# A two-layer hybrid network in one kernel: S5 output matrices made later, first loads reordered, small S5 products split, shared expert by halves

## What is computed

```python
h = layer_norm(ALPHA * h + mixed @ w_out[layer], ln1_w[layer], ln1_b[layer])
ffn = moe(h, router_w[layer], ...)          # 64 experts, 8 per token, one shared expert
h = layer_norm(ALPHA * h + ffn, ln2_w[layer], ln2_b[layer])
```

```python
shared = (jax.nn.silu(xt @ sw_gate) * (xt @ sw_up)) @ sw_down
```

## Time and profile before

| | |
|---|---|
| median of 3 executions | 1323.59 us (1323.25 to 1326.84) |
| the profiled execution | 1326.38 us |
| its span, first to last instruction | 1324.7 us |
| TensorE busy | 1287.8 us, 97% |
| TensorE weight loads | 699.5 us, 53% |
| VectorE, ScalarE, GpSimd busy | 527.7, 187.4, 46.7 us |
| mean granted TensorE clock | 0.985 of full speed |
| moved by the transfers | 462.33 MB, mean 349 GB/s |

### The profile page before, as it was taken

One profiled execution on the slowest core, in us unless ns is written; L12 is line 12 of the kernel. 1 busy time (PEld: TensorE's weight loads), 2 busy tenths in 40 slices (PEclk: granted clock), 3 DMA queues, 4 the chain that ended last, 5 costly groups with the idle time before them and its releaser, 6 DMA issues.

```text
span 1324.7 us, 16993 instructions
## 1 busy us (share of the span) xinstructions
PE 1287.8 (97%) x6753; PEld 699.5 (53%) x6753; DVE 527.7 (40%) x1071; ACT 187.4 (14%) x314; POOL 46.7 (4%) x76
## 2 busy tenths in 40 slices
PE   8979999999999999999999999999999999999996
PEld 6845564445544454445476656454445544454443
DVE  6777543333333333333336136233333333333324
ACT  3122201111111111111031212011111111111111
POOL 6200100000000000000010001000000000000000
PEclk9989999999999999999998998999999999999999
DMA  7853849999999999999952169499999999999992
GB/s 236 245 229 145 350 200 408 421 422 422 422 422 421 423 422 422 422 422 421 376 184 83 33 252 421 166 402 420 421 422 423 422 422 422 422 423 422 421 421 113
DMA packets 77625, 462.33 MB, mean 349 GB/s; under 512 B 9680, under 2 KB 10896, under 8 KB 27152
## 3 DMA queue, kind: packets, MB, share of 16 engines
q1 hardware_dynamic: 77584, 461.74, 86.0%
HBM read 455.36 MB, written 6.36 MB: 349 GB/s over the span
## 4 chain that ended last, share of the span: by engine, by line
PE 92%; DVE 4%; DMA 3%; issue 1%; ACT 1%; SPq 0%; DVEq 0%; ACTq 0%
PE bank L1040 33%; PE bank L1070 17%; PE bank L971 10%; PE bank L992 9%; PE bank L615 4%; PE bank L625 4%; PE bank L945 2%; PE bank L673 2%; PE bank L687 2%; PE bank L1051 1%; DMA expert_weights<-s_rows 1%; PE bank L1004 1%; DVE expert_weights L1531 1%; PE bank L980 1%; DMA weight_ring<-in_w_in_even 1%; PE bank L795 1%
## 5 line engine op out<-in xcount | busy, mean ns | idle before, releaser
L1070 PE MATMUL bank<-expert_weights,hiddenT 128*64 128x512 f32 x1024 | 233.8, 598 | 2.0 <-DVE hiddenT L1807 2.0
L1040 PE MATMUL bank<-expert_weights,hT 128*64 128x512 f32 x1024 | 225.3, 592 | 0.0
L1040 PE MATMUL bank<-expert_weights,weight_ring 128*64 128x512 f32 x1024 | 225.2, 592 | 0.0
L1804 DVE TENSOR_TENSOR hidden<-silu_gate,bank 128x256 f32<-128x256 f32 x64 | 26.9, 421 | 330.0 <-ACT silu_gate L1262 330.0
L1040 PEld LDWEIGHTS bank<-expert_weights,weight_ring 128*64 128x64 f32 x1024 | 74.5, 137 | 145.2 <-issue 145.2
L1040 PEld LDWEIGHTS bank<-expert_weights,hT 128*64 128x64 f32 x1024 | 73.4, 137 | 145.3 <-issue 145.0
L1070 PEld LDWEIGHTS bank<-expert_weights,hiddenT 128*64 128x64 f32 x1024 | 68.2, 136 | 119.7 <-issue 110.7
L992 PE MATMUL bank<-onehot_r,h_top 128*128 128x256 f32 x512 | 125.5, 288 | 0.0
L992 PE MATMUL bank<-onehot_r,h_low 128*128 128x256 f32 x512 | 119.7, 277 | 0.0
L971 PE MATMUL bank<-y_top,onehotT_r 128*128 128x512 f32 x264 | 111.8, 423 | 0.0
L971 PE MATMUL bank<-y_low,onehotT_r 128*128 128x512 f32 x264 | 104.5, 396 | 0.0
(11 more groups left out here) (359 smaller groups left out, 1073.6 us busy)
## 6 DMA issues: line engine op xcount, KB each, us to landing
expert_weights<-in_exp_w_gate SPq DMA_DIRECT2D x128, 1024.0 KB, 11.1
expert_weights<-in_exp_w_up SPq DMA_DIRECT2D x128, 1024.0 KB, 13.9
expert_weights<-in_exp_w_down SPq DMA_DIRECT2D x128, 1024.0 KB, 13.2
weight_ring<-in_w_in_even SPq DMA_DIRECT2D x6, 2048.0 KB, 10.3
weight_ring<-in_w_out SPq DMA_DIRECT2D x4, 2048.0 KB, 7.4
weight_ring<-in_w_in_odd SPq DMA_DIRECT2D x4, 2048.0 KB, 10.1
s_c<-expert_weights SPq DMA_DIRECT2D x1, 3072.0 KB, 8.7
expert_weights<-s_c SPq DMA_DIRECT2D x1, 3072.0 KB, 10.9
```

Of the source, the lines that this page charges most:

```text
L1040: last_mm = nc.tensor.matmul(bank[6][a * CAP:(a + 1) * CAP, :].rearrange("p (w f) -> p w f", w=2), xq[:, c, s0:s0 + CAP], ew_gu(2 * u + a, c),
L1070: last_mm = nc.tensor.matmul(bank[b][a * CAP:(a + 1) * CAP, :], hm[:, j, a * CAP:(a + 1) * CAP], ew_d(2 * u + a)[:, j, half * 512:(half + ...
L1804: nc.vector.tensor_tensor(hslot[:, :], sg[:, :], bank[6][:, DE:2 * DE], ALU.mult)\
```

## The change

- In mix0 the first loads are x tile 0, wgate, cols0, x tile 1 (the last three on the semaphore of x tile 1, waited for at 48), then xb0 and k0, and only then the other three small loads, waited for at 48 where they are read. Four warm-up products stand behind the transposes.
- `dve_s5_matrices` is split: inputs stay, `dve_s5_outputs` stands behind log_a.
- In mix1 the banks are written out by hand. K leaves the list and has the semaphore `direct`.
- The `bu` products come in two halves, the first between the halves of u's second job, the second behind `ga`. In y, r0 stands between q = 1 and q = 2 of the part from the states, instead of behind keT; ScalarE's silu of r0 moves ahead of the gelu.
- Up's second half goes to bank 2, and the shared product is made in two halves, the first behind the combine weights and ahead of the ranks' evaluation; `shared_down` has j as outer loop.
- In the ending pairs the scatter of tile 1 stands behind the transposes of the hidden part.

```diff
-                eng.wait_ge(S["x_loaded1" if t else "x_loaded"], 16)
+                eng.wait_ge(*((S["x_loaded1"], 48) if t else (S["x_loaded"], 16)))
...
 def sp_mix0(sp):
-            for dst, src in ((wgate[:, :, 0:8], ...), (cols0[:, :], A["cols_even"]), (gated..., A["lru_wa"]...),
+            for name in ("xb0", "k0"):
+                ring_load(sp, ring_no[name])
+            for dst, src in ((gated..., A["lru_wa"]...),
                              (onehotT_f..., A["lru_wx"]...), (onehot_f[:, :], A["mlstm_norm_w"]...)):
                 sp.dma_start(dst, src).then_inc(M0["params"], 16)
-            for name in ("xb0", "k0"):
-                ring_load(sp, ring_no[name])
...
-            for t, name in enumerate(("x_loaded", "x_loaded1")):
-                sp.dma_start(h[:, t, :], A["x"][0, t * P:(t + 1) * P, :]).then_inc(S[name], 16)
+            sp.dma_start(h[:, 0, :], A["x"][0, 0:P, :]).then_inc(S["x_loaded"], 16)
+            for dst, src in ((wgate[:, :, 0:8], ...), (cols0[:, :], A["cols_even"]), (h[:, 1, :], A["x"][0, P:2 * P, :])):
+                sp.dma_start(dst, src).then_inc(S["x_loaded1"], 16)
...
 def dve_mix0(dve, chain):
             last.then_inc(M0["xc"], 1)
-            dve_s5_matrices(dve, chain)
+            dve_s5_inputs(dve, chain)
             dve.wait_ge(*B.full("cols"))
...
             nc.vector.tensor_tensor(V["rg"], V["rg"], L[:, 4, :]..., ALU.mult).then_inc(M0["log_a"], 1)
+            dve_s5_outputs(dve, chain)
...
 def pe_mix1(pe):
             ring_arrived(pe, "u1")
-            for i in range(2):
-                channel_major(pe, B, ring_view("u1"), "u", i)
+            channel_major(pe, B, ring_view("u1"), "u", 0)
+            channel_half(pe, B, ring_view("u1"), "u", 1, 0)
+            pe.wait_ge(M1["b_in"], 16)
+            pe.wait_ge(*B.read("u0"))
+            for j in range(4):
+                B.wait_free(pe, f"bu{j}")
+            state_inputs((0, 1))
+            channel_half(pe, B, ring_view("u1"), "u", 1, 1).then_inc(B.full_sem, 1)
             (the gate products ga)
+            pe.wait_ge(*B.read("u1"))
+            state_inputs((2, 3))
...
             pe.wait_ge(M1["states"], 1)
             for q in range(4):
+                if q == 2:
+                    ring_arrived(pe, "r1")
+                    token_major(pe, B, ring_view("r1"), "r", 0)
...
-            ring_arrived(pe, "r1")
-            token_major(pe, B, ring_view("r1"), "r", 0)
             pe.wait_ge(*B.read("keT"))
...
 def pe_moe(pe, l):
-                        last = nc.tensor.matmul(bank[w][:, j * SEQ:(j + 1) * SEQ], wv[:, c, j, :], hT[:, c, :],
+                        dst = bank[1 + j][:, 0:SEQ] if w else bank[0][:, j * SEQ:(j + 1) * SEQ]
+                        last = nc.tensor.matmul(dst, wv[:, c, j, :], hT[:, c, :],
...
-                        scatter(1 - u, False)
+                        scatter(1 - u, False, (0,) if ending else (0, 1))
                         (transposes of hidden)
+                        if ending:
+                            scatter(1 - u, False, (1,))
...
+        def shared_hidden(dve, l, j):
+            m = MO[l]
+            dve.wait_ge(m["sh_silu"], 1)
+            dve.wait_ge(m["sh_gu"], j + 2)
+            nc.vector.tensor_tensor(shid[l][:, j, :], sh_silu[l][:, j, :], bank[1 + j][:, 0:SEQ], ALU.mult)\
+              .then_inc(m["sh_hidden"], 1)
```

More of the change, by code:

```diff
@@ L603, in _, with warm_up @@
                     pool_moe(pool, int(st[-1]))
+        def warm_up(pe, count):
+            for _ in range(count):
+                nc.tensor.matmul(bank[7][:, 0:P], ident[:, :], ident[:, :], start=True, stop=True)
         def keep_clock(pe, b, count):
@@ L608, in keep_clock, with channel_half @@
                 nc.tensor.matmul(bank[b][:, 0:SEQ], ident[:, :], hT[:, 0, :], start=True, stop=True)
-        def channel_major(pe, B, w, name, i):
[L612 to L619, removed]
+        def channel_half(pe, B, w, name, i, a):
+            if a == 0:
+                B.wait_free(pe, f"{name}{i}")
+            for c in range(KC):
+                last = nc.tensor.matmul(B.tile(f"{name}{i}")[:, a * SEQ:(a + 1) * SEQ],
+                                        w[:, c, (2 * i + a) * P:(2 * i + a + 1) * P], hT[:, c, :],
+                                        start=(c == 0), stop=(c == KC - 1))
+            return last
+        def channel_major(pe, B, w, name, i):
+            channel_half(pe, B, w, name, i, 0)
+            channel_half(pe, B, w, name, i, 1).then_inc(B.full_sem, 1)
         def token_major(pe, B, w, name, t):
@@ L657, in pe_transposes @@
                         last.then_inc(B.full_sem, 1)
+            if not stage_no[st]:
+                warm_up(pe, 4)
             for b in range(4):
@@ L783, in pe_mix1 @@
             last.then_inc(B.full_sem, 1)
-            pe.wait_ge(M1["b_in"], 16)
             pe.wait_ge(*B.read("u1"))
[L787 to L799, removed]
+            state_inputs((2, 3))
             ring_arrived(pe, "qk1")
@@ L948, in pe_moe @@
                         continue
+                    last.then_inc(m["sh_gu"], 1)
                     pe.wait_ge(m["chosen"], 1)
@@ L957, in pe_moe, with scatter @@
                 last.then_inc(m["sh_gu"], 1)
-            def scatter(par, done):
-                for t in range(TT):
+            def scatter(par, done, tiles=range(TT)):
+                for t in tiles:
                     if done:
@@ L1000, in shared_down @@
             def shared_down(t):
-                for n in range(2):
-                    for j in range(JE):
+                for j in range(JE):
+                    if t == 0:
+                        pe.wait_ge(m["sh_hidden"], j + 1)
+                    for n in range(2):
                         last = nc.tensor.matmul(bank[2 * t + n][:, :], shid[l][:, j, t * P:(t + 1) * P],
@@ L1094, in _ @@
             pe.wait_ge(S["consts"], 1)
-            for _ in range(WARM):
-                nc.tensor.matmul(bank[7][:, 0:P], ident[:, :], ident[:, :], start=True, stop=True)
+            warm_up(pe, 10)
             pe.wait_ge(S["consts"], N_CONSTS)
@@ L1182, in act_mix1 @@
                 last = nc.scalar.copy(W["direct"][rows, :, :, 32 * j:32 * j + 32],
-                                      B.tile("K")[rows, 0:384].rearrange("p (q k c) -> p q k c", q=4, k=3))
-            last.then_inc(B.done["a"], 1)
+                                      bank[1][rows, 0:384].rearrange("p (q k c) -> p q k c", q=4, k=3))
             act.wait_ge(*B.full("low"))
@@ L1200, in act_mix1 @@
                 nc.scalar.copy(W["v"][:, t, :], B.tile(f"v{t}")[:, :]).then_inc(B.done["a"], 1)
+            act.wait_ge(*B.full("r0"))
+            nc.scalar.activation(W["og"][:, 0, :], B.tile("r0")[:, :], ACT.Silu).then_inc(B.done["a"], 1)
             act.wait_ge(*B.read("y1"))
@@ L1214, in act_mix1 @@
             act_copies(act, B, "keT", W["ke_tok"])
-            for t in range(TT):
-                act.wait_ge(*B.full(f"r{t}"))
-                nc.scalar.activation(W["og"][:, t, :], B.tile(f"r{t}")[:, :], ACT.Silu).then_inc(B.done["a"], 1)
+            act.wait_ge(*B.full("r1"))
+            nc.scalar.activation(W["og"][:, 1, :], B.tile("r1")[:, :], ACT.Silu).then_inc(B.done["a"], 1)
             for i in range(2):
@@ L1527, in dve_s5_powers, with dve_s5_inputs @@
               .then_inc(M1["powers"], 1)
-        def dve_s5_matrices(dve, chain):
+        def dve_s5_inputs(dve, chain):
             mul = lambda out, x, y: nc.vector.tensor_tensor(out, x, y, ALU.mult)
@@ L1545, in dve_s5_matrices, with dve_s5_outputs @@
                 dve.wait_ge(M1["bt"], half + 1)
+        def dve_s5_outputs(dve, chain):
+            mul = lambda out, x, y: nc.vector.tensor_tensor(out, x, y, ALU.mult)
             powers = pow5[:, 0:6, :].rearrange("p (k w) n -> p k w n", w=2)
```

51 lines of the change are left out of this document (28 added, 23 removed), and 8 rows, old and new, of tables (B1, odd_jobs).

## The result

The changed kernel takes 1309.74 us (median of 4 runs, 1308.31 to 1310.14) against 1323.42 for the kernel before, run beside it: ratio 0.9884, 95% interval 0.9870 to 0.9898. It is faster by 13.7 us by the medians; the forecast was 20.4 us and 1303.2, the range 1297 to 1311. The likeliest case (1299.5 to 1307.5) did not come; what came is the rival "o0 late" (1309). The profiled execution took 1309.92 us and spans 1308.2, 16.5 less than before.

What follows compares the result with a forecast made beforehand. The prediction took TensorE, busy 97% of the span, as the bound, with gains only outside the expert loop. Its terms, 3.0 + 10.9 - 0.8 + 1.9 + 1.6 + 1.4 + 3.1 + 4.6 - 3.0 - 2.3 = 20.4 us, gave 1303.2, range 1297 to 1311.

Steps and rivals of the forecast that it cites:

- likeliest case: Whole kernel: all terms come as summed, 1303.2 us, own range 1299.5 to 1307.5; chance 0.52.
- o0 late: Rival, first mixer: store and o0's load run end to end, wait 5 to 6 us plus clock fall, 1309; chance 0.14.
- The wait for o0: First mixer: o0's load behind the output matrices' store makes TensorE wait 0.8 us, bounds 0 and 6.
- Outputs behind the decay terms: First mixer: v1's 8.63 us wait for the gate columns' copy and 2.3 of half clock go; gain 10.9 us.
- First loads: Kernel start: reordered loads let xb0's products start at 13.8 instead of 16.88; gain 3.0 us, bounds 2.0 and 3.2.
- Shared halves: Shared expert in each expert layer: making its product by halves removes shared_down's 0.94 us wait; gain 1.9 us.
- scatter: Ends of expert layers: splitting the scatter covers four 0.5 us waits for hiddenT; gain 1.6 us.
- K: L772: taking K off the bank list shortens the 2.4 us wait for its copies; gain 1.4 us.
- Small products split: Second mixer: cutting both runs of 256 removes two stops, 3.1 us, and the half clock that follows, 4.6 us.
- Slower: Rival, expert loops: the stop enters every pass, 2.2 us each, 26 us in all, 1329; chance 0.02.
- r0 ahead: Second mixer: moving r0 earlier uncovers ScalarE's work before U; loss of 3.0 us idle and 2.3 of clock.
- kinder clock: Rival: no clock fall in front of U, and one untouched fall (2.9 us) stays away, 1298; chance 0.16.

Runs made afterwards that it cites:

- o0_first: Changed kernel with the load of o0 issued ahead of the wait for the output matrices and of their store; 1304.31 us, ratio 0.9845.
- outputs_alone: Kernel before with only the S5 output matrices moved behind the decay terms; 1317.99 us, ratio 0.9948.
- before_again: Kernel before, unchanged, profiled a second time; profiled at 1323.34 us, span 1321.6.
- bu_together: Version `both` with the 256 small S5 input products in one run again, behind ga; 1303.75 us, ratio 0.9858.
- r0_back: o0_first with r0 behind the keT transposes again, so y's 256 small products are one run; 1296.69 us, ratio 0.9800.
- bu_64_192: Version `both` with the 256 small input products cut 64 and 192 instead of 128 and 128; 1297.13 us, ratio 0.9806.
- shifted_192: bu_64_192 with 36 small identity products (72 passes and their loads) added at the head of the second mixer; 1310.04 us, ratio 0.9892.
- r1_split: Changed kernel with the first four chunks of product r1 placed ahead of U, the other four behind it; 1302.25 us, ratio 0.9833.
- both: Changed kernel with the edits of o0_first and r1_split together; 1297.94 us, ratio 0.9797.
- after_again: Changed kernel, unchanged, run and profiled a second time; 1309.39 us, ratio 0.9882, span 1306.6.
- loads_alone: Kernel before with only the new order of first loads, without the warm-up products; 1321.41 us, ratio 0.9985.

## Why the prediction was right and wrong, by its steps

The time lies inside the range, but not for the reason that the sum gave: the sum missed by 6.7 us (20.4 against 13.7), and what held was that most of the rival "o0 late" had been put into the range. With the sizes measured below (first loads, outputs, o0 as in the first profile, shared halves and scatter together, K, small products, r0) the forecast's sum is 3.0 + 11.05 - 7.5 + 4.0 + 1.24 + 7.5 - 6.0 = 13.3 us, near the 13.7 measured.

**The wait for o0: the term that failed.** The step said: "I take a wait of 0.8 us, bounds 0 and 6". It was 4.98 us and 2.5 of clock in the first profile, 2.10 and 0.1 in the second. Three things went into the miss. The load took 16.2 us from issue, where I had it land 13 to 14 us after: store and load together moved 5 MB, and that is halfway between my "run together" and my "laid end to end" (19 us from the load's issue). The rival's reason, end to end, is thus only half of it, though its price came true. DVE's outputs ended at 82.6, where the step had them (85.5 less the opening's 3.0), but TensorE had come 4.7 us nearer by v0, not 3.0, as the half clock at 63 us, which the step left in, wasn't there. That makes 2.2 to 3.2 us and 1.5 us. And I put no clock fall behind the wait, though a rival had it. That it was the load's place is shown by o0_first, that it comes with this edit alone by outputs_alone.

**Outputs behind the decay terms, 10.9 us.** Right in size: from v0's start to the S products the time fell by 11.05 us (24.78 to 13.73), and the copy of the gate columns was in time.

**First loads, 3.0.** The first xb0 product came 2.98 us earlier; alone, 2.0 us by the time of the whole kernel, with 3.0 inside its interval. The step counted on the gates at full clock. That alone gives nothing: in before_again and outputs_alone they had it, and xb0 was awaited 2.05 and 2.27 us and started at 16.49 and 16.43. It's the earlier issue of xb0's load that moved the start.

**Shared halves 1.9 and scatter 1.6.** Undone together they cost 4.0 us, against 3.5 taken.

**K, 1.4.** 1.24 us: the wait is 1.21 and was 2.45.

**Small products split, 3.1 and 4.6.** Right in size, 6.5 us for bu_together and 1.0 for y's stop in r0_back, wrong in reason. I wrote that "each run is shorter than what went through before a stop". bu_64_192 let a longer one through, and shifted_192 brought the stop back at a place worked out beforehand. The stops stand at borders in the instruction stream, 256 instructions apart, with 128 small products and their loads between two borders.

The traces show what TensorE waits for there, though the profile says only "issue". Transfers of instructions go over a queue of their own, 30 of 16 KB in each profile; those of the kernel before that start in 695 to 697 us (packets, MB, share of 16 engines):

```profile
q8 instruction: 1, 0.02, 2.8%
```

It runs from 695.36 to 696.26; TensorE stops at 695.64 and goes on at 697.80. All eleven stops in these profiles, six among the input products and five among y's, are like that: an instruction transfer starts 0.3 to 1.5 us before the stop, and TensorE goes on 1.3 to 1.6 us after it has landed. In bu_64_192 none starts during the run of 192. And none starts between 291 and 605 us of the kernel before, in the hardware loop of the first expert layer, so the rival "Slower", a stop in every pass, had nothing to wait for.

A rule that I had cited beside the sum says so: the Trainium skill, page Runtime: NRT & Kernel Launch, section Instruction fetch mechanics, has the sequencer fetch blocks of 256 while it runs the present one; the runs here agree on 256. The same section calls the cost of a border mostly hidden; here it is 0.9 to 2.2 us where the block is that short. A run of 128 can't hold a whole block but by chance, so the split avoids the stop by this too. That large products in a block prevent it rests on one case, bu_64_192. What decides when a transfer starts stays open: the block of 128 input products takes 3.9 us and had stops of 1.5 to 2.2, that of y's takes 1.95 and had 0.9 to 1.5.

**r0 ahead, -3.0 and -2.3.** The wait was 2.88 us in all three profiles with that order; the half clock 3.1 to 3.3, not 2.3. This part of the edit buys 1.0 us (y's stop) and costs 6.1; r0_back shows the balance, 5.2 us. With half of r1 in the gap (r1_split) both are had.

**The clock elsewhere.** The rival "kinder clock" had an untouched fall stay away at 2.9 us: before_again shows just that, in the kernel before. That fits the first profile's place, 3.0 us above the median (1326.38 against 1323.42), and so the difference between 16.5 us by the spans and 13.7 by the medians; which falls the other executions had, no trace shows.

The best here are `both`, bu_64_192 and r0_back, 1296.7 to 1297.9, ratios 0.9797 to 0.9806, which these runs can't tell apart: 2.0% faster than before, 0.8 points more than the change.

## What to carry to other kernels

When work is moved later on one engine, follow what its result releases on a DMA queue, and what stands behind that in the program: here one load behind a 3 MB store gave back 2.2 to 7.5 us of a gain of 11, and issuing it first brought no new wait. Long runs of tiny matmuls stopped here where the transfer of the next instructions came late; count passes and weight loads in blocks of 256, and put large products between. Before a product is moved to break such a run, ask what it had covered: 6 us of cover were spent here on a stop of 1 us, and half of the next product was enough to have both.

## What the runs showed of the hardware that I had not expected

- The clock can fall without any wait. At 58 us TensorE had been busy without a break since 10 us in the changed kernel. The 16 products there took 3.9 us in 7 of the 14 profiles and 5.6 in the other 7, in the same program too. Stretches of the changed kernel's two profiles (length, engines' busy us and instructions, granted clock), the first and the second:

```profile
60.00:65.00 5.00, 5.00 (x17) 2.91 (x16) 4.93 (x5) 2.37 (x6) 0.00 (x0) 1.00 0.80 279
```

```profile
60.00:65.00 5.00, 5.00 (x15) 3.44 (x15) 4.93 (x5) 2.51 (x6) 0.00 (x0) 0.79 0.79 276
```

  The five profiles in which the first 20 products (from 1.60 us) took 4.05 to 4.37 us had no fall at 58; of the nine with 4.63 to 4.64, seven had. At the second router (about 790 us) 8 of 14 profiles had a fall, at the first (about 145 us) 2 of 14, after_again and o0_first. Why a given execution has them wasn't settled; that a wait ahead isn't needed is shown by the fall at 58.
- A wait of 2.1 us (after_again) brought no half clock behind it; those of 2.6, 4.0 and 5.0 at the same place brought 1.8, 1.8 and 2.5 us, and the 2.9 at U 3.1 to 3.3 in each of three profiles. The forecast's fall at U, taken from a wait of 3.0 us, came. But the length of the wait doesn't decide alone. The 2.45 us ahead of L772 brought none in before, before_again and loads_alone and 1.65 us in outputs_alone; ahead of xb0's first product 2.05 us brought 1.7 in before_again, and 2.27 none in outputs_alone.
- A small product isn't cheap by its columns: 64 columns cost 31 ns with 32 rows of weights (L796), and 113 ns with 128 rows and 128 columns of weights (L669 in shifted_192), at full clock. A single weight load is about as long in either form (190 ns for L796, 195 for L833, with 128 rows). L796's products take other rows in turn, four groups of 32, and their loads overlap; that this makes the difference is likely, but no run tests it.
